# Last norm's first rate by Newton steps on GpSimd, and two reorderings of TensorE work at the start of a two-block network kernel

## The reference

```python
def rms_norm(x, g):                       # the first norm, ahead of w_in
    y = xf * lax.rsqrt(jnp.mean(xf * xf, axis=-1, keepdims=True) + EPS)
p = (h @ w_in)                            # gdn_qkv, gdn_b, gdn_a, ... are slices of p
qkv = jax.nn.silu(causal_dwconv(gdn_qkv, gdn_conv_w))   # then l2norm of q and k by head

def per_layer_embed(x, p_i, g_pre, w_gate, w_proj, g_post):
    gate = jax.nn.sigmoid(rms_norm_2(x, g_pre) @ w_gate)
    return rms_norm_2(gate * (p_i @ w_proj), g_post)
x = x + per_layer_embed(...)              # of the second layer: the last thing computed
```

## Time and profile before

| what | us |
| --- | --- |
| median of 3 runs | 1015.68 (1014.24, 1016.24, 1015.68) |
| the profiled execution's own time | 1014.75 |
| its span in the trace | 1012.9 |
| PE busy | 999.3 |
| DVE busy | 846.0 |
| ACT busy | 618.7 |
| POOL busy | 5.8 |

### The profile page before, as it was taken

How to read it: one execution, slowest core, us unless ns; L and a number is a source line. 1 busy time by engine, 2 the same in 40 slices (tenths; PEclk the granted TensorE clock), 3 DMA queues, 4 the chain that set the end, 5 groups by cost and what they waited for, 6 DMA issues and landing times.

```text
span 1012.9 us, 20813 instructions
## 1 busy us (share of the span) xinstructions
PE 999.3 (99%) x8343; PEld 935.8 (92%) x8343; DVE 846.0 (84%) x1217; ACT 618.7 (61%) x852; POOL 5.8 (1%) x16
## 2 busy tenths in 40 slices
PE   8999999999999999999999999999999999999996
PEld 7998999999999998899999999999999999999985
DVE  6974896899988878869999888799776899988876
ACT  6753565657565655457565556675676666555565
POOL 0000000000000000000000000000000000000000
PEclk9999999999999999999999999999999999999998
DMA  8533315455555545657656555345445356655531
GB/s 328 185 117 96 126 48 176 166 206 172 209 202 171 202 149 184 208 209 231 213 172 209 203 173 201 125 167 184 150 132 174 129 173 210 209 201 186 187 125 42
DMA packets 26498, 175.99 MB, mean 174 GB/s; under 512 B 3229, under 2 KB 3509, under 8 KB 6080
## 3 DMA queue, kind: packets, MB, share of 16 engines
q1 hardware_dynamic: 25616, 171.31, 48.6%
q0 software_dynamic: 816, 3.73, 1.3%
HBM read 173.97 MB, written 2.63 MB: 174 GB/s over the span
## 4 chain that ended last, share of the span: by engine, by line
PE 84%; DVE 7%; ACT 3%; issue 2%; DMA 2%; SPq 0%; DVEq 0%; ACTq 0%
PE PS L587 71%; PE PS L538 12%; DVE w_lo L2244 2%; ACT w_hi L1503 2%; DMA arena<-masks_in 1%; DMA raw<-weights 1%; DVE arena L3051 1%; DVE arena L3024 1%; DVE arena L2385 1%; PE PS L1408 0%; DVE arena L3062 0%; DVE arena L2795 0%; DVE arena L3061 0%; DVE arena L3045 0%; DVE arena L3041 0%
## 5 line engine op out<-in xcount | busy, mean ns | idle before, releaser
L587 PE MATMUL PS<-h_store,w_hi 128*128 128x256 f32 (+1 forms) x1840 | 478.2, 338 | 1.3 <-DVE w_lo L2299 0.9
L2244 DVE TENSOR_TENSOR w_lo<-raw,w_hi 128x2048 fp32r<-128x2048 f32 x154 | 352.5, 2290 | 52.4 <-ACT w_hi L1503 47.2
L587 PE MATMUL PS<-h_store,w_lo 128*128 128x256 f32 (+1 forms) x1400 | 369.5, 281 | 0.2
L1503 ACT ACTIVATE w_hi<-raw 128x2048 fp32r<-128x2048 f32 x156 | 297.9, 1910 | 79.1 <-PE PS L587 64.4
L587 PEld LDWEIGHTS PS<-h_store,w_hi 128*128 128x128 f32 x1840 | 305.3, 187 | 41.0 <-DVE w_lo L2299 1.3
L587 PEld LDWEIGHTS PS<-h_store,w_lo 128*128 128x128 f32 (+1 forms) x1400 | 254.8, 188 | 0.8 <-DVE h_store L2858 0.6
L587 PE MATMUL PS<-act_hi,w_hi 128*128 128x256 f32 x704 | 195.7, 280 | 0.1
L587 PE MATMUL PS<-act_hi,w_lo 128*128 128x256 f32 x704 | 195.1, 279 | 0.1
L587 PE MATMUL PS<-act_lo,w_hi 128*128 128x256 f32 x704 | 192.0, 279 | 0.0
L587 PEld LDWEIGHTS PS<-act_hi,w_hi 128*128 128x128 f32 x704 | 132.3, 188 | 1.6 <-DVE act_hi L2858 0.6
L587 PEld LDWEIGHTS PS<-act_hi,w_lo 128*128 128x128 f32 x704 | 132.3, 188 | 0.3 <-DVE act_hi L2858 0.3
(11 more groups left out here) (361 smaller groups left out, 1106.6 us busy)
## 6 DMA issues: line engine op xcount, KB each, us to landing
raw<-weights SPq DMA_DIRECT2D x155, 1024.0 KB, 4.9
raw<-weights SPq DMA_DIRECT2D x12, 256.0 KB, 3.9
arena<-masks_in SPq DMA_DIRECT2D x1, 1600.0 KB, 12.1
bias_by_key<-bias_by_distance POOLq DMA_DIRECT2D x1, 1536.0 KB, 8.0
x<-x_in SPq DMA_DIRECT2D x4, 256.0 KB, 4.4
raw<-weights SPq DMA_DIRECT2D x2, 512.0 KB, 9.0
arena<-bias_by_key POOLq DMA_DIRECT2D x1, 1024.0 KB, 6.7
result<-arena SPq DMA_DIRECT2D x4, 256.0 KB, 2.1
```

The source lines that it names most:

```text
L587: return pe.matmul(o, lhs, rhs, start=start, stop=stop, skip_group_check=True)
L1503: act.activation(w_hi[:, slot, :], raw[:, slot, :], ACT.Copy).then_inc(hi_ready, 1)
L2244: tt(w_lo[:, slot, :], raw[:, slot, :], w_hi[:, slot, :].bitcast(F), ALU.subtract).then_inc(lo_ready, 1)
```

## The change

Three edits.
- GpSimd computes the rate of token tile 0. DVE makes the mean square and a first guess of its reciprocal root from the bits of the number (`first_guess`); GpSimd then does three Newton steps in twelve instructions of 128 x 1, each linked to the next (`first_rstd`). ACT drops `rstd(0)`; `square(3)` stands right behind the table load, and the second tile's Ln and Exp behind it. DVE's `result(0)` moves ahead of `product(3)`, and waits for `first_rstd`; `bias(0)` becomes linked.
- `gdn_tokens((0, 1), 1)` moves from behind to ahead of `project(5, 0)`.
- In `first_columns` the small products of chunk 3 stand behind chunk 4, those of 4 and 5 behind chunk 5, that of 6 behind chunk 6, that of 7 behind chunk 7.

```diff
@@ -84,6 +84,8 @@
              ("v", 1), ("v", 2), ("v", 3))
 ATT_BANK = (4, 5, 7, 1, 5, 4, 5, 4, 5, 4, 5, 4)
 T_PARTS = 5
+LAST_POST = 5
+ROOT_GUESS = float(0x5F3759DF)
 WIDE = 1 + 2 * (PAIRS - 3)
 SC_WIDE = 9
 SC_BANKS = ((4, 5, 6), (0, 2, 4), (6, 0, 2), (0, 4, 6))
@@ -430,6 +432,7 @@
         gain_row = v_tok[:, 0, :]
         by_quarter = prod.rearrange("p c n -> p (c n)").rearrange("p (b n) -> p b n", b=4)
         sum_of_squares, norm_bias, norm_r = (att_stat[0][:, a:b] for a, b in ((0, 4), (4, 6), (6, 8)))
+        mean_square, half_square, root, step = (att_stat[0][:, a:a + 1] for a in range(8, 12))
 
         def hi_at(p, c):
 
@@ -529,6 +532,22 @@
             pool.dma_start(p_tok, p_in[1]).then_inc(sem("p_loaded"), 16)
             pool.wait_ge(sem("heads_out"), 4)
             pool.dma_start(gain_row, last_gain_in.partition_broadcast(P)).then_inc(sem("table_loaded"), 16)
+
+            def first_rstd(q):
+
+
+                tt, ts = pool.tensor_tensor, pool.tensor_scalar
+                pool.wait_ge(sem("y_sum"), y_sum(q, 1))
+                link(ts(half_square, mean_square, 0.5, None, ALU.mult))
+                for n in range(3):
+                    link(tt(step, root, root, ALU.mult))
+                    link(tt(step, step, half_square, ALU.mult))
+                    link(ts(step, step, -1.0, 1.5, ALU.mult, ALU.add))
+                    if n < 2:
+                        link(tt(root, root, step, ALU.mult))
+                tt(norm_r[:, 0:1], root, step, ALU.mult).then_inc(sem("first_rstd"), 1)
+
+            first_rstd(LAST_POST)
 
 
 
@@ -833,6 +852,8 @@
             def first_columns():
 
 
+                SMALL_BEHIND = ((), (), (0,), (1,), (2, 3), (4, 5), (6,), (7,))
+
                 def small_products(k):
                     if k == 0:
                         block_ready(0)
@@ -858,11 +879,8 @@
                             last = add(o, w_hi[:, 1, at], a[:, k, :], k == 0 and f == 0 and lo == 0, k == KC - 1 and lo == 1)
                             if lo == 0:
                                 add(o, w_lo[:, 1, at], a[:, k, :])
-                    if k >= 2 and k < KC - 1:
-                        small_products(k - 2)
-                small_products(KC - 3)
-                small_products(KC - 2)
-                small_products(KC - 1)
+                    for kk in SMALL_BEHIND[k]:
+                        small_products(kk)
                 last.then_inc(block_used, 1)
 
             def turn_small():
@@ -1227,8 +1245,8 @@
             gates()
             project(4, 0)
             project(4, 1)
+            gdn_tokens((0, 1), 1)
             project(5, 0)
-            gdn_tokens((0, 1), 1)
             project(5, 1)
             gdn_tokens((2,), 2)
             project(6, 0)
@@ -2082,14 +2100,6 @@
                     act.activation(sq4[:, b, :], by_quarter[:, b, :], ACT.Square, accum_out=sum_of_squares[:, b:b + 1]) \
                         .then_inc(sem("y_squares"), 1)
 
-                def rstd(t):
-
-                    act.wait_ge(sem("y_squares"), y_square(q, 2 * t + 2))
-                    act.wait_ge(sem("y_sum"), y_sum(q, t + 1))
-                    r = norm_r[:, t:t + 1]
-                    link(act.activation(r, sum_of_squares[:, 2 * t + 1:2 * t + 2], ACT.Ln, scale=1.0 / D, bias=norm_bias[:, t:t + 1]))
-                    act.activation(r, r, ACT.Exp, scale=-0.5).then_inc(sem("y_rstd"), 1)
-
                 act.wait_ge(sem("x_rstd"), 8)
                 gate_sigmoid(0)
                 gate_sigmoid(1)
@@ -2099,9 +2109,12 @@
                 square(2)
                 gate_sigmoid(3)
                 act.preload_act_table_set(TABLES)
-                rstd(0)
                 square(3)
-                rstd(1)
+                act.wait_ge(sem("y_squares"), y_square(q, 4))
+                act.wait_ge(sem("y_sum"), y_sum(q, 2))
+                r = norm_r[:, 1:2]
+                link(act.activation(r, sum_of_squares[:, 3:4], ACT.Ln, scale=1.0 / D, bias=norm_bias[:, 1:2]))
+                act.activation(r, r, ACT.Exp, scale=-0.5).then_inc(sem("y_rstd"), 1)
 
             def product_squares(b):
 
@@ -3145,14 +3158,25 @@
 
                 def bias(t):
                     dve.wait_ge(sem("y_squares"), y_square(q, 2 * t + 1))
-                    ts(norm_bias[:, t:t + 1], sum_of_squares[:, 2 * t:2 * t + 1], 1.0 / D, EPS, ALU.mult, ALU.add) \
-                        .then_inc(sem("y_sum"), 1)
+                    ins = ts(norm_bias[:, t:t + 1], sum_of_squares[:, 2 * t:2 * t + 1], 1.0 / D, EPS, ALU.mult, ALU.add)
+                    if t:
+                        ins.then_inc(sem("y_sum"), 1)
+                    else:
+                        link(ins)
+
+                def first_guess():
+                    dve.wait_ge(sem("y_squares"), y_square(q, 2))
+                    link(stt(mean_square, sum_of_squares[:, 1:2], 1.0 / D, norm_bias[:, 0:1], ALU.mult, ALU.add))
+                    ts(root.bitcast(I32), mean_square.bitcast(I32), -0.5, ROOT_GUESS, ALU.mult, ALU.add).then_inc(sem("y_sum"), 1)
 
                 def result(b):
-                    if b % 2 == 0:
+                    if b == 0:
                         settle()
-                        dve.wait_ge(sem("y_rstd"), q + b // 2 + 1)
+                        dve.wait_ge(sem("first_rstd"), 1)
                         dve.wait_ge(sem("mixed_turned"), 4 + 4)
+                    if b == 2:
+                        settle()
+                        dve.wait_ge(sem("y_rstd"), q + 1)
                     stt(by_quarter[:, b, :], quarter(z[b]), norm_r[:, b // 2:b // 2 + 1], PS[:, 4 + b, :], ALU.mult, ALU.add) \
                         .then_inc(x_chunk, 1)
 
@@ -3163,13 +3187,16 @@
                 gain(0)
                 bias(0)
                 gain(1)
+                first_guess()
                 product(2)
                 gain(2)
                 bias(1)
+                result(0)
                 product(3)
                 gain(3)
-                for b in range(4):
-                    result(b)
+                result(1)
+                result(2)
+                result(3)
 
             ffn_and_ple(0, 3, 1)
             fold_sum(sum_x)
```

## The result

The changed kernel took 1016.13 us (median of 12 executions, 1015.48 to 1018.55), the kernel before 1014.50 (12 executions, 1013.56 to 1016.24): a ratio of 1.0020, with a 95% interval of 1.0011 to 1.0028. It is slower by 0.1% to 0.3%, some 2 us by the ratio and 1.63 us by the medians; I had forecast 0.47 us less. (Three executions of over 2,000 us, one each in two of the later runs and one of the kernel before beside them, are in no ratio.) The profiled execution of the changed kernel is one of its three longest (1018.55 us, span 1016.8), 3.9 us over the span of before.

The account below looks back on a forecast made before the run. TensorE's unchanged work was taken to bound the kernel. The front edits' -0.06 and the end's -0.41 sum to -0.47 us, from 1015.68 to 1015.2 us, called no change; range 1013.7 to 1017.6.

Parts of the forecast that it names:

- The bound: Whole kernel: TensorE's unchanged work bounds it, busy 999.3 of 1012.9 us; only the idle 13.6 us can give time.
- small products: Ahead of chunk 6: moved small products fill TensorE's 0.21 us wait; local worth 0 to 0.21 us.
- delta tokens: Block 5: transposes put ahead of its high products remove TensorE's 0.40 us wait for the low part; local worth 0.40.
- What is late next: Blocks 6 and 7: TensorE, 0.61 us early, waits for DVE's low parts, 0.35 us at block 6; -0.06 us survives.
- The end's formula: Last norm: the end shifts by T - 1006.17, never below -0.57 us, as product 3 stands behind result 0.
- T: Time when GpSimd's rate of token tile 0 is ready: 1003.36 + 12 x 0.20 = 1005.76, giving -0.41 us.
- Blocking by product 2 and gain 2: End: DVE's products might hold GpSimd back, making the shift +0.78 us instead of -0.41; left out of the sum.
- The step length: GpSimd's chain: s, the time per linked step, taken as 0.20 us from DVE's small step; bounds 0.13 and 0.40.
- GpSimd's rate is late by a little, by the port or by s from 0.24 to 0.32: Rival at the end: result 0 passes the delay on, +0.1 to +1.9 us, some 1016.5; chance 0.36.
- The rival that was to be slower past 0.2%: End: T past 1008.26, by s over 0.41, or over 0.32 with blocking; up to 1018.6 us; chance 0.12.
- Result 0 ahead of product 3: End, DVE's order: result 0 waits for GpSimd and passes each delay on to product 3, square 3 and second rate.
- The slower rule on freshly loaded code: GpSimd's chain: a first call to freshly loaded code pays some 6 us, making the end about 5.6 us later.

Follow-up runs that it names:

- the run with GpSimd alone: Changed kernel with DVE's product 2 waiting for GpSimd's rate, so GpSimd's chain runs beside no VectorE work; one execution, 1016.77 us.
- the run with the early masks: Kernel before with the masks' transfer issued ahead of block 3's; 1017.87 us, ratio 1.0025 to the kernel before.

## Why the prediction was wrong

**The bound, small products, delta tokens: right.** No wait stands ahead of chunk 6 or block 5 in the new start. What is late next was right as well: 0.36 us at block 6, where I had 0.35 (0.21 to 0.36 us in the other profiles with the new start in which the masks came in time). Against the start of block 7's low part on VectorE, TensorE's low products begin 2.34 us later with the new start (53.62 - 51.28) and 2.37 us with the old one: the two front edits give 0.03 us of the 0.61 us of waits that they remove at their own place, for a forecast of 0.06. The ratio of the start edits alone, 1.0002, agrees and can't see so small a term.

**The end's formula: right.** I had the shift as T - 1006.17 from the time T of GpSimd's rate. In the changed kernel T is 1009.81 + 0.19 = 1010.00, and 1007.70 with the 2.30 us of later start taken off; the formula then says +1.53 and the trace +1.60, a difference within the 0.1 us to which a span is given. As the formula has it, ACT's second rate sets the end: it is ready at 1012.77 (1012.57 + 0.20), and result 2 waits for it, so that the last three results take 2.19 us for 2.06 (0.74 + 2 x 0.66).

**T itself: wrong, and this is the step that failed.** I had T = 1003.36 + 12 x 0.20 = 1005.76; it was 1007.70, 1.94 us later. Term by term:
- GpSimd starts at 1003.41 in that frame, +0.05.
- Blocking by product 2 and gain 2, at nothing in my sum: +0.77. The first two steps take 0.68 us each (1005.71 to 1006.39 to 1007.07), for 0.32 and 0.27 in the run with GpSimd alone. I had put it outside the sum because no row of before showed the two engines together, and left it to a rival. The Trainium skill's rule (SBUF — State Buffer, Who interferes with whom), that a VectorE instruction with two SBUF inputs contends with a GpSimd instruction that reads SBUF, agrees with every trace here: instructions of 0.19 us became 0.49 to 0.67 beside products and gains, and GpSimd alone had none. That one input would not block is hardly tested: the only case is bias 1 (1007.00 to 1007.15), beside which GpSimd's third instruction kept its 0.19. The clear that only writes couldn't have shown it.
- The step length, 0.20 in my sum: +0.93. With GpSimd alone the twelve distances between the thirteen starts are 3.33 us (1006.15 - 1002.82), 0.277 each, for 2.40. Of that 0.19 is the instruction and 0.08 the hand-over to itself, where VectorE needs 0.15 and 0.03 to 0.04. I took VectorE's row as the nearest in kind; GpSimd's own linked row, 0.40 (a clear of 33 x 8, not of one column), was the upper bound, and the truth lay between them.
- The count: +0.19. The chain has thirteen instructions, not the twelve of my text and my sum; twelve are linked, and the thirteenth adds its own 0.19.

These are the 1.94 us (0.05 + 0.77 + 0.93 + 0.19). Without the blocking T would have been 1006.93 (1003.41 + 3.52), and the end later all the same, by an estimated 0.76 us (1006.93 - 1006.17).

So the case that came is the rival "GpSimd's rate is late by a little, by the port or by s from 0.24 to 0.32", to which I gave the same chance as to the forecast. Of its two causes both held (0.277 lies in its range for s), and with both the end shift came to 1.60 us. That the time I named, 1015.2 us, is only 0.9 below the measured median is luck: its base, the median of three executions, was 1.18 above the median of twelve (1015.68 - 1014.50). The rival that was to be slower past 0.2% needed T past 1008.26, and T was 1007.70. The measured ratio touches 0.2% all the same; the end's 1.60 us are 0.16%, inside the intervals of both measurements (1.0011 to 1.0028 and 1.0004 to 1.0023) and of the end's edit alone (1.0003 to 1.0021). What the first measurement has above it fits the three executions near 1018.5 us (the mean of the nine others is 1.3 us above the mean of before), one of which the profile shows with late masks and a halved clock; no run settles why they came in that one.

**Result 0 ahead of product 3: right as a mechanism.** Moving it behind gain 3 gave 0.54 us of the stretch back (9.43 to 8.89), less than the formula's 1.5, since the freed product 3 and gain 3 blocked GpSimd in turn.

**The slower rule on freshly loaded code: not seen.** Of the 6 us that the Trainium skill gives for the first call to freshly loaded code (GPSIMD Engine Reference, Instruction dispatch) no trace shows anything; the first tensor_scalar took 0.23 us with VectorE silent. Whether any code was freshly loaded here, no run shows.

## What to carry to other kernels

Moving a short chain of small dependent operations to an idle engine pays by the step length of that engine, not by its idleness: here instructions 0.27 us apart on GpSimd lost to instructions 0.2 to 0.3 us apart that VectorE could fit into its own idle time. The length and the place of the chain weighed more than the engine (1.08 and 0.54 us for 0.36, undone in that order), so count its instructions in the code, every one, before pricing it. Before placing GpSimd work that reads SBUF, list the VectorE instructions with two SBUF inputs that run beside it, and add each one's remaining time to the chain; here two of them cost 0.77 us. And an instruction that waits on an uncertain chain should not stand in front of one that feeds another engine; when a wait is removed, look two blocks ahead for the producer that is only just in time.

## What I had not expected of the hardware

- After an idle time of 1.31 us TensorE's granted clock was 0.52 for the next 3.5 us, and sixteen products took 3.69 us for 2.1; after 1.19 us in another kernel they took 2.13. The two differ by little in the gap and wholly in what follows, and behind a wait of 3.09 us in the run with the early masks the clock stayed at 1.00. Ahead of the first two gaps TensorE had only eight small products of 8 columns each, from 30.41 and 30.08 us on, ahead of the third full ones. So the length of the gap alone doesn't tell, and what made the clock fall stays open.
- The landing of one 1.6 MB transfer, issued at 11.5 to 11.8 us in seven of the profiles, moves between 23.4 and 25.8 us there, with the DMA engines full, and ACT's and DVE's next work waits for it.
- A VectorE operation of one column with two scalars read from SBUF takes 0.27 us, for 0.15 with constants.
